# Differential mixer: turned weights times values in single true float32 products, the output squared right behind its copy

## The reference, cut to what matters

```
sc = q[:, qs:qe] . k[:, :qe] * HEAD_DIM ** -0.5 + bias     # for two maps m, causal by chunks of 64
pr = softmax(sc)
a  = pr[:, :, 0] - lam * pr[:, :, 1]
o  = a @ v[:, :qe]                                          # (128 queries) x (128 value columns)
o  = rms_norm(o, subln_g) * (1 - lambda_init)
```

## Time and profile before

| | us |
|---|---|
| median of 3 runs | 1228.64 |
| lowest, highest | 1228.44, 1233.47 |
| span of the profiled execution | 1229.7 |
| PE busy in it | 1197.1 |
| DVE busy | 867.3 |
| ACT busy | 517.8 |
| POOL busy | 250.2 |

### The profile page before, as it was taken

How to read it: one execution, slowest core, us unless ns; L and a number is a source line. 1 busy time by engine, 2 the same in 40 slices (tenths; PEclk the granted TensorE clock), 3 DMA queues, 4 the chain that set the end, 5 groups by cost and what they waited for, 6 DMA issues and landing times.

```text
span 1229.7 us, 17128 instructions
## 1 busy us (share of the span) xinstructions
PE 1197.1 (97%) x6167; PEld 1001.8 (81%) x6167; DVE 867.3 (71%) x1514; ACT 517.8 (42%) x1045; POOL 250.2 (20%) x291
## 2 busy tenths in 40 slices
PE   8999999999888999999999999999999999999997
PEld 7998887788676888888888888888888888888886
DVE  5433786877886577877787777877777999964443
ACT  4312665565655224433343343343344444733321
POOL 0000000344455122232332323323210000000000
PEclk9999999999899999999999999999999999999999
DMA  7464233111831512242322333233499533620101
GB/s 217 89 90 91 50 89 76 42 40 69 222 139 42 164 52 81 82 128 94 121 87 89 125 103 112 95 94 112 146 345 312 172 95 103 225 75 26 43 35 51
DMA packets 127916, 136.08 MB, mean 111 GB/s; under 512 B 15714, under 2 KB 93274, under 8 KB 127770
## 3 DMA queue, kind: packets, MB, share of 16 engines
q1 hardware_dynamic: 127834, 135.00, 36.1%
HBM read 96.77 MB, written 37.22 MB: 109 GB/s over the span
## 4 chain that ended last, share of the span: by engine, by line
PE 61%; issue 4%; DVE 2%; POOL 1%; ACT 1%; POOLq 0%; DVEq 0%; ACTq 0%
PE ps L1723 60%; PE ps L1729 1%; DVE xs L1474 1%; DVE h L1469 0%; DVE conv L1410 0%; POOL stat L687 0%; ACT xs L796 0%; DVE act_t L1185 0%; POOL stat L706 0%; POOL bias_a L712 0%; POOL more_f L714 0%; PE ps L2118 0%; ACT wbuf L793 0%; POOL o_t L709 0%; DVE h L1688 0%
## 5 line engine op out<-in xcount | busy, mean ns | idle before, releaser
L1723 PE MATMUL ps<-act_t,wbuf 128*128 128x512 f32 x1200 | 280.1, 389 | 0.5 <-DVE a_buf L1499 0.5
L1723 PEld LDWEIGHTS ps<-act_t,wbuf 128*128 128x128 f32 x1200 | 225.2, 188 | 47.5 <-DVE a_buf L1499 0.8
L1723 PE MATMUL ps<-wbuf 128*128 128x512 f32 x912 | 214.8, 390 | 0.0
L1723 PEld LDWEIGHTS ps<-wbuf 128*128 128x128 f32 x912 | 170.6, 188 | 35.1
L1723 PE MATMUL ps<-act_t,wq 128*128 128x512 f32 x624 | 152.2, 396 | 3.6 <-DVE wq L1187 3.0
L1723 PEld LDWEIGHTS ps<-act_t,wq 128*128 128x128 f32 x624 | 114.3, 188 | 30.8 <-issue 7.5
L687 POOL TENSOR_TENSOR stat<-stat 128x1 f32<-128x1 f32 x32 | 17.6, 549 | 420.9 <-DVE stat L1194 420.9
L793 ACT ACTIVATE wbuf<-raw 128x512 fp32r<-128x512 f32 (+1 forms) x107 | 69.0, 646 | 73.9 <-PE ps L1723 63.8
L1723 PE MATMUL ps<-hx,wbuf 128*128 128x512 f32 x408 | 95.7, 389 | 0.0
L1185 DVE TENSOR_TENSOR wbuf<-raw,wbuf 128x512 fp32r<-128x512 f32 (+1 forms) x107 | 87.4, 818 | 11.5 <-ACT wbuf L793 11.2
L1723 PEld LDWEIGHTS ps<-hx,wbuf 128*128 128x128 f32 x408 | 76.5, 188 | 15.9
(11 more groups left out here) (208 smaller groups left out, 1962.8 us busy)
## 6 DMA issues: line engine op xcount, KB each, us to landing
u_ops<-wbuf_f SPq DMA_DIRECT2D x77, 256.0 KB, 2.2
raw<-u_ops SPq DMA_DIRECT2D x77, 256.0 KB, 2.7
raw<-in_w_ffn_in SPq DMA_DIRECT2D x33, 512.0 KB, 3.8
g_ffn<-in_w_ffn_in SPq DMA_DIRECT2D x11, 512.0 KB, 3.9
act_f<-in_w_ffn_out SPq DMA_DIRECT2D x21, 256.0 KB, 4.3
w_raw<-in_w_in SPq DMA_DIRECT2D x10, 512.0 KB, 4.4
wbuf_f<-in_w_ffn_out SPq DMA_DIRECT2D x18, 256.0 KB, 5.9
x_in<-in_x SPq DMA_DIRECT2D x8, 512.0 KB, 3.8
```

Of the source, the lines that this page charges most:

```text
L1723: return nc.tensor.matmul(dst, lhs, rhs, start=start, stop=stop)
```

## The change

1. `v_b` holds the values once, as float32, 128 columns for each key tile and head, and a tile `spare` takes the place that the low halves had. ACT copies three heads (L835), DVE copies the fourth; the low halves are no longer made.
2. The turned weights are copied whole to a float32 tile `a_f`, which lies where `a_t` lies and holds two blocks, by one ACT copy. DVE's low half goes. ACT's copy waits for the product of the block before the last in place of the last. The semaphores `b_thi` and `b_tlo` become one, `b_copied`.
3. The product with v is one float32 matmul of 128 columns for each key tile in place of two float32r ones.
4. ACT copies one 128-column output and squares it straight from PSUM right behind the copy, ahead of the exponentials. POOL's sum and its semaphore `b_sum` go. `o_sb` is used in two halves by turns.
5. DVE's low half of a turned output waits for `b_copied`, so that it doesn't read a bank beside ACT's copy.

```
-    v_b = sb(attn, "v_b", [P, NT, BH, 2 * P], F32R)
+    v_b = sb(attn, "v_b", [P, NT, BH, P])
+    spare = sb(attn, "spare", [P, 4 * D])
...
+    a_f = sb(whole, "a_f", [P, 2, SEQ])
...
# POOL
             pool.wait_ge(S.b_part, n + 1)
+            pool.wait_ge(S.b_sq, n + 1)
             if n >= 1:
                 pool.wait_ge(S.b_y, n)
-            nc.gpsimd.tensor_tensor(o, o_sb[:, 0, :], o_sb[:, 1, :], ALU.add).then_inc(S.b_sum, 1)
-            pool.wait_ge(S.b_sq, n + 1)
...
-            link(nc.gpsimd.tensor_scalar(o, o, stat[:, st + 2:st + 3], None, ALU.mult))
+            link(nc.gpsimd.tensor_scalar(o, o_sb[:, n % 2, :], stat[:, st + 2:st + 3], None, ALU.mult))
...
# ACT
-                nc.scalar.activation(v_b[:, u, 0:3, 0:P], ps[:, 4 + u % 2, 0:V_CUT].rearrange("p (h n) -> p h n", h=3),
+                nc.scalar.activation(v_b[:, u, 0:3, :], ps[:, 4 + u % 2, 0:V_CUT].rearrange("p (h n) -> p h n", h=3),
                                      ACT.Copy)
-                nc.scalar.activation(v_b[:, u, 3, 0:P], ps[:, 6 + u % 2, 0:P], ACT.Copy)
...
                 act.wait_ge(S.b_turned, m + 1)
-                if m >= 1:
-                    act.wait_ge(S.b_pv, m)
+                if m >= 2:
+                    act.wait_ge(S.b_pv, m - 1)
+                if m == 0:
+                    act.wait_ge(S.a_pv, NA)
                 if m == 4:
                     act.wait_ge(S.a_stored, 32 * NA)
-                copy(a_t[:, 0, 0:w], psf[:, 5 * HALF:5 * HALF + w], S.b_thi)
+                copy(a_f[:, m % 2, 0:w], psf[:, 5 * HALF:5 * HALF + w], S.b_copied)
...
                 act.wait_ge(S.b_pv, m + 1)
-                if m >= 1:
-                    act.wait_ge(S.b_sq, m)
+                if m >= 2:
+                    act.wait_ge(S.b_y, m - 1)
                 act.wait_ge(S.b_diff, m + 1)
                 col = 4 * (m % 4)
-                nc.scalar.activation(o_sb[:, :, :], ps[:, 7, 0:2 * P].rearrange("p (a q) -> p a q", a=2), ACT.Copy,
-                                     scale=small[:, col:col + 1]).then_inc(S.b_part, 1)
+                o = ps[:, 7, 0:P]
+                copy(o_sb[:, m % 2, :], o, S.b_part, small[:, col:col + 1])
+                nc.scalar.activation(sq_out, o, ACT.Square, scale=small[:, col:col + 1],
+                                     accum_out=stat[:, 16 + 3 * (m % 2):17 + 3 * (m % 2)]).then_inc(S.b_sq, 1)
...
-            if 3 <= n <= NBS + 2:
-                m = n - 3
-                act.wait_ge(S.b_sum, m + 1)
-                square(o_t[:, :], sq_out, stat[:, 16 + 3 * (m % 2):17 + 3 * (m % 2)], S.b_sq)
...
# DVE
-                low(v_b[:, u, 0:3, P:2 * P], ps[:, 4 + u % 2, 0:V_CUT].rearrange("p (h n) -> p h n", h=3),
-                    v_b[:, u, 0:3, 0:P], None)
-                low(v_b[:, u, 3, P:2 * P], ps[:, 6 + u % 2, 0:P], v_b[:, u, 3, 0:P], None)
+                nc.vector.tensor_copy(v_b[:, u, 3, :], ps[:, 6 + u % 2, 0:P])
...
             if m >= 4:
-                dve.wait_ge(S.b_part, m - 3)
+                dve.wait_ge(S.b_sq, m - 3)
...
-            if 2 <= n <= NBS + 1:
-                m = n - 2
-                w = P * (m % NT + 1)
-                dve.wait_ge(S.b_thi, m + 1)
-                low(a_t[:, 1, 0:w], psf[:, 5 * HALF:5 * HALF + w], a_t[:, 0, 0:w], S.b_tlo)
             for m in turned_with(n - 1):
                 dve.wait_ge(S.b_yhi, turned_with(n - 1)[-1] + 1)
+                dve.wait_ge(S.b_copied, min(n - 1, NBS))
                 low(mix_dst(m, 1), y_bank(n - 1, m), mix_dst(m, 0), S.b_ylo)
...
# PE
             if 2 <= n <= NBS + 1:
-                pe.wait_ge(S.b_tlo, n - 1)
+                pe.wait_ge(S.b_copied, n - 1)
...
-                pe.wait_ge(S.b_tlo, m + 1)
+                pe.wait_ge(S.b_copied, m + 1)
                 if m >= 1:
-                    pe.wait_ge(S.b_part, m)
+                    pe.wait_ge(S.b_sq, m)
                 for k in range(nk):
-                    mm(ps[:, 7, 0:2 * P], a_t[:, 0, k * P:(k + 1) * P], v_b[:, k, hb, :], k == 0, False)
-                    ins = mm(ps[:, 7, 0:P], a_t[:, 1, k * P:(k + 1) * P], v_b[:, k, hb, 0:P], False, k == nk - 1)
+                    ins = mm(ps[:, 7, 0:P], a_f[:, m % 2, k * P:(k + 1) * P], v_b[:, k, hb, :],
+                             k == 0, k == nk - 1)
                 ins.then_inc(S.b_pv, 1)
```

More of the change, by code:

```diff
@@ L119, in build @@
     e_t = sb(attn, "e_t", [P, 2, 2, SEQ])
+    whole = ExitStack()
+    a_f = sb(whole, "a_f", [P, 2, SEQ])
+    whole.close()
     a_t = sb(attn, "a_t", [P, 2, SEQ], F32R)
@@ L271, in build @@
     a_scores a_logits a_exp a_probs a_turned a_thi a_tlo a_pv a_ohi a_olo
-    b_scores b_max b_exp b_diff b_turned b_thi b_tlo b_pv b_part b_sum b_sq b_y b_yturned b_yhi b_ylo
+    b_scores b_max b_exp b_diff b_turned b_copied b_pv b_part b_sq b_y b_yturned b_yhi b_ylo
     wo_hi wo_lo mix_c mix_45 mix_23 c_done c_added oproj h_mid sq1 ms1 pow1 xs1_ready tr1 xhi1 xlo1 gffn_in o_row
```

## The result

| | before | after |
|---|---|---|
| median, same rounds, 4 runs each (us) | 1229.62 | 1219.13 |
| lowest, highest | 1228.44, 1233.47 | 1218.80, 1220.26 |
| span of the profiled execution | 1229.7 | 1217.2 |

The ratio is 0.9916, with a 95% interval of 0.9902 to 0.9930: the change takes off 8.6 to 12.1 us, 10.5 by the medians. 1216.4 was forecast, with a range of 1210 to 1223. The profiled run took 1219.04, so 1.84 us lie outside its span; the forecast had put the span at 1229.7 − 12.2 = 1217.5. Of the 2.7 us between 1219.13 and 1216.4, 1.0 lies in the base: the median before was 1228.64 when the forecast was made.

What follows compares the result with a forecast made beforehand. TensorE, busy 97% of the span, was taken as the bound, so other savings count only through its waits. Mixer 8.5, end 1.35, clock 1.7 and product 0.7 sum to 12.2 us: 1228.6 to 1216.4, range 1210 to 1223.

Steps and rivals of the forecast that it cites:

- The mixer, 8.5: Differential mixer: removing VectorE's low halves shortens the VectorE-ScalarE loop where TensorE is bare, 2.8 + 5.3 + 0.4 us saved.
- The 0.95 taken off: Late mixer blocks: 0.95 us deducted from the loop's saving where the shortened loop falls below TensorE's own work.
- The product, 0.7: Turned weights times values: two float32 passes replace 0.229 us per key tile; 0.7 us saved over 144 tiles.
- Rival 1: Product: weight loads exposed in each pass, 0.49 us per key tile, 38 us more TensorE work, 1249 us; chance 0.06.
- rival 2: Product: columns decide its cost, 7.7 us more instead of 0.7 less, 1224.8 us; chance 0.05.
- The turning point of 0.31 us per key tile: Product: the cost per key tile above which the change would make the kernel slower, 0.229 + 12.2/144.
- The output path: Mixer output: ScalarE squares early, GpSimd's sum goes; its 3.5 us of waits vanish, no extra gain, no new wait costs.
- The end, 1.35: Mixer's end: last turn waits 1.0 us less, plus 0.35 of a further 0.9 us; 1.35 us saved.
- the slack at w_out's last row: Mixer's end: w_out's last row ready at 408.3, asked for at about 408.7; under 0.4 us, so 0.35 counted.
- The clock, 1.7: Behind the last turn: with half its wait left, the 3.41 us half-speed stretch was expected to vanish, saving 1.7 us.
- Rival 3: Mixer: ScalarE takes the loop over or scores are late, half of 8.5 us lost, clock falls again, 1222; chance 0.14.
- rival 4: Mixer: becomes full TensorE work and both half-speed stretches vanish, 1210 us; chance 0.12.

Runs made afterwards that it cites:

- low_back: Changed kernel with a VectorE operation of the removed low half's width put back at its old place, yielding nothing used; 1231.51 us, ratio 1.0012.
- product_twice: Changed kernel with each block's product of turned weights and values done twice, the second over the first; 1244.16 us, ratio 1.0108.
- square_back: Changed kernel with ScalarE's square behind the exponentials again, read from the output's SBUF copy; 1221.05 us, ratio 0.9929.
- after_again: Changed kernel repeated without edits, in the same rounds as a repeat with w_out's last row block fetched early; 1220.74 us, ratio 0.9933.
- all_back: Changed kernel with a low-half-width VectorE operation, the square behind the exponentials, and ScalarE's weights copy waiting for the previous block's product; 1229.88 us, ratio 0.9994.
- no_high_low: Kernel before the change with the first product 128 columns wide instead of 256, except in block 0; 1232.78 us, one run.
- before_again: Kernel before the change, unedited, run for a second profile; 1230.28 us.
- row3_early: Changed kernel with w_out's last row block fetched early into a free place of `spare`; 1216.45 us, ratio 0.9889.
- gain_later: Changed kernel with the feed-forward gain's transfer held back until w_out's last row has landed; 1220.59 us, ratio 0.9918.

## Why the prediction was right, and where it was not

**The mixer, 8.5.** Right, in its cause and nearly in its size. Blocks 0 to 19 gave 3.2 us (2.8 forecast), blocks 20 to 31 5.5 (5.3, with the 0.4 of block 27 5.7). low_back, which adds that operation alone, loses 3.2 and 5.65. No exponentials are waited for around blocks 7 and 15, as was said; PE's waits but for w_out's come to 8.7 us and not to about 7; 1.1 of the difference are the two waits at output turns near blocks 20 and 21 on DVE's low half, that were not foreseen. One argument of this term was wrong, though little hung on it: 5.7 and 4.3 us of idle time are 10.0, and loops that lose 6.2 don't nearly use them up; 6.7 us stayed in the mixer. The 0.95 taken off for it was a guess that came out near.

**The product, 0.7.** This term was mis-sized: nothing was saved. The pace was right: 0.112 a pass is inside the range of 0.107 to 0.116, and the old pair costs 0.230 a key tile, near the 0.229 used. What the sum left out is a cost once in each block. The first true pass starts 0.109 us behind the last transpose and not 0.028, and the work behind the product starts 0.205 behind the last pass and not 0.152. From the last transpose to the work behind, a block of one key tile takes 0.424 us for 0.384, one of eight 1.988 for 1.995. Over all 32 blocks the new product is some 0.5 us dearer, an estimate from such rows. Rival 1 (0.49 a key tile) and rival 2 (three passes at their columns) fall. The Trainium skill (TensorE: Matmul & The Clock Gate, LDWEIGHTS) puts a load at about its columns over 1.2 in ns, an estimate of 107 for 128 columns, and the traces' 0.112 a pass lies just above it. The four passes that the prediction drew from the Trainium skill (FP8 and Floating Point Precision, TensorE Precision Notes) count the way through the array and give no price; no run here shows the split's three at their columns. The turning point of 0.31 us per key tile was not measured: product_twice, at 0.447, is slower than before, and a straight line between it and the kernel after crosses before's time at 0.32, an estimate from their medians.

**The output path at nothing.** Right. square_back puts POOL's waits back and costs 0.6 in the mixer, inside the 0 to 1.2 expected. Its median is 1.9 us over the kernel after, in other rounds; its profiled start and rest hold 3.6 of the 4.5 us by which its span is longer, and both have a half-speed stretch that the kernel after lacks.

**The end, 1.35.** The 1.0 at the turn came (2.07 to 1.08). The step that failed is the slack at w_out's last row. It said that the wait there would be 0.55; it was 2.40, 2.57 in after_again. Two things add up. PE's own way from the issue of the transfers to that row fell from 16.0 us (392.70 to 408.7) to 14.57 (379.02 to 393.59), 1.4 to 1.5 and not 0.9. Of that, 0.9 are the two waits that were counted (0.71 and 0.23); where the rest comes from is open. And the transfers took longer: from that issue to ACT's split 13.2 us before, 14.6 after. Of ten traces with this order, those of before, all_back, no_high_low and product_twice have 13.2 to 13.4, the other six 14.4 to 14.8, before_again among them (14.42, in its rows above). So both values belong to the same kernel, and the forecast had taken the lower one for a constant. In nine of the ten mixer A's rows had landed by 12.1 to 12.3 us, and what differs is w_out's row, 1.1 or 2.2 to 2.5 behind them; in before_again mixer A's rows themselves were at 13.4. Against before_again the end is 2.4 us shorter. row3_early shows the cost from the other side: with the row in place beforehand, 2.6 us go.

**The clock, 1.7.** Right in the profile, and not certain. The half-speed stretch behind the last turn is gone, and it is in none of the traces with a turn wait of about 1.1. But a wait of 2.1 isn't enough to bring it: before, before_again and low_back have the wait and the stretch, all_back (2.06) and no_high_low (2.09) have the wait and the full clock. So the forecast's 1.7 was a saving in three of five executions, put in as certain. The rows of before_again and, in the second fence, of all_back:

```profile
385.40:388.80 3.40, 3.40 (x17) 3.37 (x16) 0.00 (x0) 0.56 (x3) 1.90 (x5) 0.50 0.00 0
```

```profile
386.00:390.00 4.00, 3.56 (x27) 3.42 (x28) 2.23 (x4) 0.82 (x1) 3.17 (x6) 1.00 0.01 2
```

And the new wait at w_out's last row can bring a stretch of its own, as in after_again, where the rest is 1.5 us longer than in the kernel after:

```profile
397.00:400.40 3.40, 3.40 (x10) 2.62 (x9) 1.22 (x1) 1.12 (x2) 0.00 (x0) 0.50 1.02 291
```

It stands in three of five traces with a wait of 2.3 to 2.6 there (after_again, gain_later, square_back), not in after and low_back. So a part of the 1.7 is often given back. The stretch in the bare loop, costed at nothing, costs little where it is short: after has 3.4 us of it and after_again has none, and their mixers are 164.2 and 164.0, since the idle time is 6.7 and 8.0. With 13.6 us of it no_high_low's mixer is 2.1 longer than before's.

**The sum.** 12.2 were forecast. Of the profile's 12.5, 2.4 are chance at the start, and 10.1 remain: 8.7 in the mixer, 1.5 behind it. So it is luck that the profiled span, 1217.2, lies beside the 1217.5 forecast. The medians' 10.5 agree with the 10.1 and are 1.7 under the forecast, which is about the end's shortfall (3.05 to 1.5); after_again's 7.9 lies lower. Rival 3 (ACT takes the loop over) falls by the 5.93 us of the loop, rival 4 by the 6.7 us of idle time left in the mixer.

Open: why w_out's row lands after 13.2 or 14.6 us, why the same wait brings half speed in one execution and not in another, and why the same kernel after is 10.5 us under before in one set of rounds and 7.9 in another.

## What to carry to other kernels

Find the operation that lies inside the loop of two engines and take its duration off only where the third engine is bare; the wait's name in a list is no guide to its price, since one removed wait hands its time to the next. A split product of small tiles can be paced by its instructions and not by its columns. Then a true float32 product costs about the same (0.223 for 0.230 a key tile here, and some 0.05 once in a block), and both splits are saved. When a stage gets shorter, every transfer issued in it loses cover: look at the spread of such a transfer over several executions before counting on a slack of less than a microsecond.

## What the runs showed of the hardware

- A true float32 product of 128 by 128 by 128 is recorded as two passes 0.112 us apart, 0.223 in all. Two float32r products with 128 weight columns each took 0.223 with 128 moving columns each, and 0.230 with 256 and 128.
- A first true float32 pass behind float32 transposes started 0.109 us behind the last of them, a first float32r product 0.028.
- Four 512 KB transfers with one more of 512 KB behind them took 13.2 to 13.4 us or 14.4 to 14.8 from issue to the landing of the last, in executions of the same kernel too.
- The start of this kernel, up to block 1, took 208.4 to 211.9 us whatever was changed behind it. The spans of two single executions can't tell differences below 3.5 us; the cuts by stage can.
